# Attention: normalising the probabilities through a diagonal matrix on TensorE in place of scaling the rows on VectorE

## The reference, cut to what matters

```python
scores = jnp.where(valid, scores, NEG_INF)
m = jnp.max(scores, axis=-1, keepdims=True)
p = jnp.exp(scores - m)
den = jnp.sum(p, axis=-1, keepdims=True)
out = jnp.einsum("brhnqk,brhnkc->brhnqc", p.astype(v.dtype), v_band)
out = out / den.astype(out.dtype)
lse = (m + jnp.log(den))[..., 0]
...
wts = jax.nn.softmax(jnp.stack(lses, axis=0), axis=0)
merged = jnp.sum(wts[..., None].astype(outs.dtype) * outs, axis=0)
```

## Time and profile before

| | |
|---|---|
| median of 3 runs | 2382.86 us (2381.7 to 2383.41) |
| the profiled execution's own time | 2385.08 us |
| its span | 2383.3 us |
| TensorE busy | 2316.8 us, 97% of the span |
| VectorE busy | 770.5 us, 32% |
| ScalarE busy | 418.4 us, 18% |
| DMA, mean over the span | 256 GB/s |
| attention, from the first transpose to the end of the first unit of "o" | 635.62 to 683.4 us of the span |

### The profile page before, as it was taken

How to read it: one execution, slowest core, us unless ns; L and a number is a source line. 1 busy time by engine, 2 the same in 40 slices (tenths; PEclk the granted TensorE clock), 3 DMA queues, 4 the chain that set the end, 5 groups by cost and what they waited for, 6 DMA issues and landing times.

```text
span 2383.3 us, 31423 instructions
## 1 busy us (share of the span) xinstructions
PE 2316.8 (97%) x12958; PEld 1747.2 (73%) x12958; DVE 770.5 (32%) x1885; ACT 418.4 (18%) x1026; POOL 0.2 (0%) x4
## 2 busy tenths in 40 slices
PE   8999999999999999999999999999999999999998
PEld 7888888888888888888887787555555555555544
DVE  7734374210434421100355823222222222222212
ACT  5332202010242211100024402111111111111111
POOL 0000000000000000000000000000000000000000
PEclk9999999999999999899999999999999999999999
DMA  6134476654324443234332377999999999999996
GB/s 268 43 133 159 144 296 232 228 222 185 107 89 143 158 148 135 71 115 142 78 125 89 129 285 280 404 427 427 429 428 428 428 428 428 428 428 428 428 427 288
DMA packets 59599, 611.27 MB, mean 256 GB/s; under 512 B 6856, under 2 KB 8264, under 8 KB 10224
## 3 DMA queue, kind: packets, MB, share of 16 engines
q1 hardware_dynamic: 59504, 609.93, 64.4%
HBM read 606.74 MB, written 1.06 MB: 255 GB/s over the span
## 4 chain that ended last, share of the span: by engine, by line
PE 77%; DMA 15%; DVE 7%; issue 1%; ACT 1%; SPq 0%; DVEq 0%; ACTq 0%
PE bank L628 28%; PE bank L1178 14%; PE bank L625 8%; DMA arena<-in_experts 7%; DMA ring<-in_experts 7%; PE bank L716 5%; PE bank L1204 4%; PE bank L642 3%; DVE arena L1809 3%; PE bank L617 2%; PE bank L1169 2%; PE bank L1137 1%; PE bank L727 1%; PE bank L1125 1%; PE bank L747 1%
## 5 line engine op out<-in xcount | busy, mean ns | idle before, releaser
L628 PE MATMUL bank<-arena,ring 128*128 128x256 f32 x3264 | 711.0, 380 | 0.0
L628 PEld LDWEIGHTS bank<-arena,ring 128*128 128x128 f32 x3264 | 622.7, 191 | 83.7
L2240 DVE TENSOR_SCALAR arena<-bank 128x256 f32<-128x256 f32 x64 | 27.2, 425 | 675.4 <-PE bank L1178 675.4
L1178 PE MATMUL bank<-arena 128*64 128x256 f32 x2048 | 231.3, 381 | 14.2 <-DMA arena<-in_experts 14.2
L1178 PE MATMUL bank<-ring,arena 128*64 128x256 f32 x2048 | 233.4, 383 | 5.8 <-DMA ring<-in_experts 5.8
L1178 PEld LDWEIGHTS bank<-ring,arena 128*64 128x64 f32 x2048 | 143.0, 137 | 111.1 <-issue 28.7
L1178 PEld LDWEIGHTS bank<-arena 128*64 128x64 f32 x2048 | 144.4, 137 | 102.9 <-DMA arena<-in_experts 22.5
L625 PE MATMUL bank<-ring,arena 128*128 128x256 f32 x896 | 194.0, 380 | 1.0 <-issue 1.0
L625 PEld LDWEIGHTS bank<-ring,arena 128*128 128x128 f32 x896 | 170.4, 190 | 24.1 <-issue 1.4
L716 PE MATMUL bank<-arena,ring 128*128 128x256 f32 x576 | 124.6, 379 | 0.0
L716 PEld LDWEIGHTS bank<-arena,ring 128*128 128x128 f32 x576 | 109.6, 190 | 14.7
(11 more groups left out here) (301 smaller groups left out, 1905.3 us busy)
## 6 DMA issues: line engine op xcount, KB each, us to landing
arena<-in_experts SPq DMA_DIRECT2D x96, 2048.0 KB, 32.4
ring<-in_experts SPq DMA_DIRECT2D x95, 2048.0 KB, 30.9
ring<-in_dense SPq DMA_DIRECT2D x186, 1024.0 KB, 4.8
ring<-arena SPq DMA_DIRECT2D x16, 128.0 KB, 5.8
con<-in_con SPq DMA_DIRECT2D x1, 1248.0 KB, 12.0
X<-in_x SPq DMA_DIRECT2D x1, 1024.0 KB, 4.9
arena<-in_cond SPq DMA_DIRECT2D x1, 1024.0 KB, 17.5
arena<-in_ctx SPq DMA_DIRECT2D x1, 1024.0 KB, 4.8
```

The lines of the kernel that those rows point to most:

```text
L628: ins = nc.tensor.matmul(o, w[:, k, j * P:(j + 1) * P], src[:, k, :], start=(k == 0), stop=(k == KT - 1))
L1178: ins = nc.tensor.matmul(o, XGT[:, k, e * CAP:(e + 1) * CAP], w[:, k, :], start=False, stop=(k == KT - 1), skip_group_check=True)
```

## The change

`scaled(h)` no longer multiplies the probabilities. It multiplies the 128x128 identity by the column of reciprocal sums, once for each part, into a new tile `A_DG` (four such matrices, two for each parity of the head). The nine transposes of a head become nine ordinary products of the block of `A_P` with that diagonal matrix, so that transposing and scaling come out of one product. The order of the instructions on every engine, the semaphores and the waits stay as they are. `A_DG` takes 512 columns of the arena that are free in this stage.

```diff
@@ -271,6 +271,7 @@
         A_SM = [area(NB + 23040 + 16 * i, 16) for i in range(2)]
+        A_DG = tiles(area(NB + 23080, 512), 4)
@@ -767,8 +768,9 @@
                         if h and not to and n % 4 == 0:
                             pe.wait_ge(sem("att_pt"), 3 * (h - 1) + n // 4 + 1)
-                        ins = nc.tensor.transpose(banks[to + n // 4][:, (n % 4) * P:(n % 4 + 1) * P],
-                                                  A_P[h % 2][:, n * P:(n + 1) * P], ident)
+                        ins = nc.tensor.matmul(banks[to + n // 4][:, (n % 4) * P:(n % 4 + 1) * P],
+                                               A_P[h % 2][:, n * P:(n + 1) * P], A_DG[:, h % 2 * 2 + n // 6, :],
+                                               start=True, stop=True, skip_group_check=True)
                         if n in (3, 7, 8):
                             ins.then_inc(sem("att_tr"), 1)
@@ -1731,11 +1733,11 @@
                 def scaled(h):
-                    Pm, sm = A_P[h % 2], A_SM[h % 2]
-                    for i, (a, b) in enumerate(((0, 768), (768, 1152))):
+                    sm = A_SM[h % 2]
+                    for i in range(2):
                         dve.wait_ge(sem("att_exp"), 2 * h + i + 1)
                         me(V.reciprocal(sm[:, 6 + i:7 + i], sm[:, 4 + i:5 + i]))
-                        V.tensor_scalar(Pm[:, a:b], Pm[:, a:b], sm[:, 6 + i:7 + i], None, ALU.mult)\
+                        V.tensor_scalar(A_DG[:, h % 2 * 2 + i, :], ident, sm[:, 6 + i:7 + i], None, ALU.mult)\
                          .then_inc(sem("att_p"), 1)
```

## The result

The changed kernel takes 2390.27 us (median of 11 executions, 2387.8 to 2392.53) beside 2382.48 us for the kernel before (2381.59 to 2384.97, also 11). The ratio is 1.0031, with an interval of 1.0023 to 1.0039: slower, by 0.31%. The profiled execution took 2389.43 us, its span 2387.6 us.

A forecast was written before the change was run, and what follows sets the result against it. Attention was taken as bound by a chain alternating between TensorE and VectorE. Head 0 -0.335, six periods +3.79, head 6 +0.85 and head 7 +0.97 sum to +5.3 us: 2388.1 us, range 2385.6 to 2390.6 (some 8 in 10).

The forecast's parts named there:

- TensorE's step: Attention, each head: nine products take 2.007 us where nine transposes took 1.04, +0.967 us a head.
- The spacing of 0.1115 us: TensorE's new products: 18 instructions a head, each starting 0.1115 us after the one before, as in L790.
- The diagonal: VectorE's scaling of the 128-column identity: 286 ns, making the first scaling of a head 0.335 us shorter.
- The period: Attention, steady part: one head takes 6.17 us instead of 5.54, +0.632 us, six times, +3.79 us.
- Head 0: Start of the attention: head 0's transposes wait for the same scaling and start 0.335 us earlier.
- Head 6: Late in the attention: no scores hide the copies, so the values start later, +0.85 us.
- The covers: Attention: ScalarE's later copies and exponentials still finish in time, with more than a microsecond to spare.
- The delay reaches the end: Stages behind the attention: the expert-weight stream starts when TensorE frees buffers, so all 5.3 us pass on.
- the rival of a swallowed delay: Expert stage: a weight stream that does not move absorbs the delay, +0 us, 2382.9 us; chance 6%.
- that products cost no more than transposes: Attention on TensorE: equal cost, seven starts 0.335 us earlier, -2.3 us, 2380.5 us; chance 5%.
- that they cost four times as much: Attention on TensorE: nine products take 4.16 us for 1.04, +22.6 us, 2405.5 us; chance 3%.
- That all weight loads come into the open: Attention on TensorE: load and product no longer overlap, 192 ns per instruction, +17 us, 2399.9 us; chance 4%.

The follow-up runs named there:

- experiment 3: The kernel before with 16 idle products ahead of head 0's transposes: 2389.78 us beside 2382.32, ratio 1.0029.
- experiment 4: The kernel before, transposes kept, with ScalarE scaling the first 768 columns and VectorE making their reciprocal ahead of the masking: 2377.48 us beside 2382.32, ratio 0.9980.
- spread gates: The changed kernel with half a unit of the next stage behind each eight gate products: 2385.34 us, ratio 1.0009 to the kernel before.

## Why the prediction was right, and where it was off

The mechanism was right but for one thing, the slow start of a group of products, and the sum of +5.3 us was too small by 0.7. The result lies in the range, 0.3 us below its upper end, and that it does is partly luck: the upper end was there for a diagonal of 420 ns or a spacing of 0.125 us, neither of which came, and it had no place for the term that did. Of the 7.8 us between the first medians the trace explains 6.0.

- **TensorE's step** is the term that was mis-sized. The prediction had +0.967 us a head. Measured are +1.07 us where the group starts after a wait (2.11 us from 641.29 to 643.40, against 1.04) and +1.03 us at head 7, where it does not (2.01 us against 0.98). The spacing of 0.1115 us was right: 18 of them are the 2.01 us of head 7. The error was to set a group of transposes after a wait (1.04 us, the slow start in it) against products in full stream. The trace had head 7's transposes at 0.98 us in the earlier trace rows, and the 0.06 us between the two was the sign. With products the slow start costs 0.10 us. The trace of the kernel before had this price as well: the six instructions of L785 that waited for ScalarE in head 6 take from 670.81 us to 671.58 (the row below), so 0.77 us, where six in a stream take 0.67. I put it down to the first weight load, which stands in the open and takes 192 ns where a transpose's takes 141; the sizes fit, but no run isolates it.

```profile
671.58 1.50 PE L790 MATMUL bank<-arena 128*128 128x128 f32 x12
```

- **The diagonal** was forecast at 286 ns, and measured at 286.
- **The period** came out at 6.27 us for 6.17, all of it from the step above, six times 0.10. Part by part the trace has 2.11 (products) + 2.17 + 1.55 + 0.10 + 0.29 + 0.05 us, so only the first term is off. The period is 0.29 us above the 5.98 us that TensorE needs alone: the 0.19 us of the forecast and the 0.10 of the slow start.
- **Head 0** starts 1.23 us behind `q_out(11)` for 1.56, -0.33 us as forecast. **Head 6** costs 675.55 + 2.12 - 672.66 = 5.01 us against 4.10, +0.91 for +0.85.
- With these sizes the prediction's sum reads -0.33 + 6 x 0.735 + 0.91 + 1.03 = +6.0 us, the 6.02 of the trace. From its first product on the attention is 6.35 us longer (635.05 to 689.55 against 635.62 to 683.77 us), for 5.6 in the forecast.
- **The covers** held: the copies ended before the values in all heads but head 6, and the second, shorter scaling freed nothing.
- **The delay reaches the end**: experiment 3 shows it for a bare delay. The reason given holds too. The queue's first long issue of expert weights comes at 1423.32 us before and at 1425.80 after, 2.5 us later, as TensorE itself is behind by then, and TensorE's wait for them stays at 14.2 us (L1180, L1178 before). So the rival of a swallowed delay falls.
- **The rivals**: that products cost no more than transposes, and that they cost four times as much, fall by the same row (2.01 against 0.98 us). That all weight loads come into the open falls by the spacing of 0.1115 us; by the reading above it is true of the first of a group that starts after a wait.

The advice of the Trainium skill ("Perfetto Trace Analysis", section "Transposes") to use a transpose and no standard matmul holds here: the nine products in full stream take 2.05 times the transposes. The Trainium skill, "TensorE: Matmul & The Clock Gate", section "Terms", calls the transpose mode 4x faster for 32-bit data, and no run here shows more than this 2.05.

What stays open is small. The first comparison gave 7.8 us between the medians, the trace 6.0. With all executions taken together the means differ by 6.6 +- 0.4 us, so 0.6 us are left, 1.3 standard errors. I take it for chance in how long the half clock lasts. That executions with a lower mean clock take longer is shown, but not that it makes these 0.6 us: with the mean clock taken into account by a straight line the two kernels still differ by 6.6 +- 0.3 us.

## What to carry to other kernels

Before work goes from VectorE to TensorE, count TensorE's instructions: a 32-bit product is two where a transpose is one, so folding a scale into a transpose doubles that step on the engine that was the bound. A wait behind an engine with a low busy share can be a matter of order: here the scaling stood behind the masking in one queue, and giving it to the engine that was idle at that time (experiment 4) won more than VectorE's shortened work did, at no cost to TensorE. When a group's time is read from a row, see whether it started after a wait, and compare only like with like.

## What was not expected of the hardware

TensorE's clock fell from 2.4 to 1.2 GHz while its matmul row showed it busy without a pause, in a row of products with 16 moving columns, and stayed there for 7 to 14 us. With eight wide products of 256 columns (3.5 us) behind each eight narrow ones (1.7 us) it did not fall, worth 4.5 us of the whole kernel for a change of order alone. Executions of one program differ by up to 7 us (the kernel before, 2379.2 to 2386.18), at least in part by stretches of this kind. That is more than the effect under study, so the trace's own stage, which came out at 55.73 us in three traces of the changed kernel (one of them with spread gates), gave the size of this change better than the medians of ten executions did.
